# One plain fp32 weight tile at each norm in place of two, and a later start for GpSimd's rows

## The reference, cut to what matters

```python
for l in range(DEPTH):                                   # DEPTH = 2
    h = layer_norm(ALPHA * h + 0.5 * swiglu(h, ffn1_gate[l], ffn1_up[l], ffn1_down[l]), ln_g[l, 0], ln_b[l, 0])
    z = h @ w_in[l]
    ...
    mix = jnp.concatenate([y_conv, y_rec, y_pool], axis=-1) @ w_out[l]
    h = layer_norm(ALPHA * h + mix, ln_g[l, 1], ln_b[l, 1])
    h = layer_norm(ALPHA * h + cross_attn(h, mem, ca_q[l], ca_k[l], ca_v[l], ca_o[l]), ln_g[l, 2], ln_b[l, 2])
    h = layer_norm(ALPHA * h + 0.5 * swiglu(h, ffn2_gate[l], ffn2_up[l], ffn2_down[l]), ln_g[l, 3], ln_b[l, 3])
```

## Time and profile before

| | |
|---|---|
| runs | 2506.68, 2508.70, 2508.75 us, median 2508.7 |
| the profiled execution | 2508.65 us, span 2506.9 us |
| TensorE busy | 2435.2 us, 97% |
| VectorE, ScalarE, GpSimd busy | 1107.7, 827.6, 211.9 us |
| granted TensorE clock, mean | 0.99 of full speed |

### The profile page before, as it was taken

How to read it: one execution, slowest core, us unless ns; L and a number is a source line. 1 busy time by engine, 2 the same in 40 slices (tenths; PEclk the granted TensorE clock), 3 DMA queues, 4 the chain that set the end, 5 groups by cost and what they waited for, 6 DMA issues and landing times. The chain is left out here.

```text
span 2506.9 us, 36308 instructions
## 1 busy us (share of the span) xinstructions
PE 2435.2 (97%) x15029; PEld 1790.5 (71%) x15029; DVE 1107.7 (44%) x1434; ACT 827.6 (33%) x955; POOL 211.9 (8%) x100
## 2 busy tenths in 40 slices
PE   8999999999999999999999999999999999999996
PEld 8999988999999998899999954444444444444442
DVE  4557766644645867654578741112111111212112
ACT  4344344433433434433446411212222211222120
POOL 0002402200200331110020010000000000000001
PEclk9999999999999999999999999999999999999997
DMA  7665454565565545456455557999999999999990
GB/s 241 210 202 168 136 184 151 169 202 181 172 201 172 169 149 185 134 186 202 152 182 166 165 209 315 428 427 430 428 428 428 429 429 428 430 427 429 428 423 18
DMA packets 215307, 665.16 MB, mean 265 GB/s; under 512 B 9841, under 2 KB 164207, under 8 KB 190624
## 3 DMA queue, kind: packets, MB, share of 16 engines
q1 hardware_dynamic: 214912, 662.53, 69.5%
q10 hardware_dynamic: 288, 1.05, 0.1%
HBM read 662.50 MB, written 1.05 MB: 265 GB/s over the span
## 5 line engine op out<-in xcount | busy, mean ns | idle before, releaser
L598 PE MATMUL ps<-ring_halves 128*128 128x256 f32 x5984 | 753.3, 284 | 0.0
L598 PEld LDWEIGHTS ps<-ring_halves 128*128 128x128 f32 x5984 | 734.2, 192 | 3.5 <-issue 0.6
L1803 DVE TENSOR_TENSOR ring_halves<-ring,ring_halves 128x2048 fp32r<-128x2048 f32 x206 | 511.5, 2491 | 360.9 <-ACT ring_halves L1320 360.8
L1320 ACT CAST ring_halves<-ring 128x2048 fp32r<-128x2048 f32 x206 | 391.2, 1903 | 276.1 <-PE ps L598 141.6
L1192 PE MATMUL ps<-ring,work 128*64 128x512 f32 x2048 | 452.3, 596 | 22.8 <-DMA ring<-in_w_up_dram 22.0
L1308 ACT COPY work<-ps 128x512 f32<-128x512 f32 x190 | 109.6, 586 | 840.9 <-PE ps L1192 390.7
L1192 PEld LDWEIGHTS ps<-ring,work 128*64 128x64 f32 x2048 | 145.8, 137 | 323.3 <-issue 269.5
L2305 DVE TENSOR_SCALAR work<-work 128x128 f32<-128x128 f32 x64 | 19.3, 344 | 610.1 <-PE ps L1192 610.1
L609 PE MATMUL ps<-ring_halves,work_halves 128*128 128x512 f32 x1184 | 288.4, 391 | 0.0
L2424 POOL TENSOR_TENSOR h<-hn,work 128x1024 f32<-128x1024 f32 x20 | 79.6, 3980 | 2084.9 <-DVE hn L1843 1052.9
L609 PEld LDWEIGHTS ps<-ring_halves,work_halves 128*128 128x128 f32 x1184 | 219.7, 188 | 44.4 <-issue 0.5
(11 more groups left out here) (257 smaller groups left out, 1736.0 us busy)
## 6 DMA issues: line engine op xcount, KB each, us to landing
ring<-in_w_up_dram SPq DMA_DIRECT2D x128, 2048.0 KB, 23.7
ring<-in_w_down_dram SPq DMA_DIRECT2D x64, 2048.0 KB, 19.3
ring<-in_w_in_dram SPq DMA_DIRECT2D x52, 1024.0 KB, 5.2
ring<-in_ffn_gate_dram SPq DMA_DIRECT2D x44, 1024.0 KB, 5.4
ring<-in_ffn_up_dram SPq DMA_DIRECT2D x44, 1024.0 KB, 5.3
ring<-in_ffn_down_dram SPq DMA_DIRECT2D x44, 1024.0 KB, 4.9
ring<-in_w_out_dram SPq DMA_DIRECT2D x12, 1024.0 KB, 4.9
ring<-in_ca_k_dram SPq DMA_DIRECT2D x8, 1024.0 KB, 5.1
```

The lines of the kernel that those rows point to most:

```text
L598: mm = pe.matmul(ps[:, bank, pt * T:pt * T + T], wt[:, o:o + P], x[:, k, :], start=(k == 0 and n == 0), stop=(k == DT - 1 and n == 2))
L1320: nc.scalar.copy(high_of(name)[:], ring[:, s, :]).then_inc(hi_done.add(name), 1)
L1803: v.tensor_tensor(ring_halves[s][:], ring[:, s, :], high_of(name)[:].bitcast(F32), ALU.subtract)\
```

## The change

At each of the eight norms only tile a is left in plain fp32. Tile b (`rf1`, `cq1`, `up 0`, `xa1`) joins the split tiles: it gets its place at the head of the order, ScalarE and VectorE prepare it, and TensorE multiplies it by `by_columns` after both halves are there. The first feed-forward stage of layer 0, which has no norm before it, keeps its way. GpSimd's rows wait for the low half of tile b and no longer for the split of the inputs.

```diff
+ORDER_MIX1 = ("rf1", "rq0", "rq1", "cc", "ch", "cb", "pu", "ri0", "ri1", "ck0", "ck1", "ck2", "ck3", "rg0", "rg1",
+              "cv0", "cv1", "cv2", "cv3", "wo0", "wo1", "wo2", "wo3", "cq1", "cq2", "cq3", "co0", "co1", "co2", "co3")
+ORDER_MIX2 = ("xa1", "xa2", "xa3", "q0", "q1", "k0", "k1", "v0", "v1", "v2", "v3", "go0", "go1", "go2", "go3",
...
-    out = []
+    out = [] if tag == ("f1", 0) else [(tag, "up", 0)]
...
                 half(a_name, a_bank, 0, (0, 1))
-                open_bank(b_bank, b_name)
-                arrived(b_name)
-                half(b_name, b_bank, 0, (0,))
                 transposes(tag, 1, hn)
-                half(b_name, b_bank, 0, (1,))
                 turned_copied(tag, 1)
                 release(half(a_name, a_bank, 1, (0, 1)), a_name)
-                release(half(b_name, b_bank, 1, (0, 1)), b_name)
+                split_inputs(tag)
+                by_columns(b_name, b_bank)
...
                     slot_used(act, (f"rf{j}", L))
                     nc.scalar.activation(work[:, FQ + 512 * j:FQ + 512 * j + 512], ps[:, j, :], ACT.Sigmoid)\
                         .then_inc(emptied[j].sem, 1)
+                next_high(("rf1", L))
...
                 mine(("k", L))
+                next_low(("rf1", L))
                 next_low(("rq0", L))
                 next_low(("rq1", L))
...
                 negmax(1)
+                next_low(("cq1", L))
                 next_low(("cq2", L))
                 normalise(1)
...
             conv(0)
+            next_low("xa1")
             next_low("xa2")
...
                 if tag[0] not in ("A", "B"):
-                    pool.wait_ge(dve_done.sem, dve_done.at(("xlow", tag, 1)))
+                    n, L = tag
+                    second = {0: ("rf1", L), 1: ("cq1", L), 2: (("f2", L), "up", 0),
+                              3: (("f1", L + 1), "up", 0) if L + 1 < LAYERS else "xa1"}[n]
+                    pool.wait_ge(lo_done.sem, lo_done.at(second))
```

More of the change, by code:

```diff
@@ L156, in join @@
             ln.n = n
-ORDER_MIX1 = ("rq0", "rq1", "cc", "ch", "cb", "pu", "ri0", "ri1", "ck0", "ck1", "ck2", "ck3", "rg0", "rg1",
-              "cv0", "cv1", "cv2", "cv3", "wo0", "wo1", "wo2", "wo3", "cq2", "cq3", "co0", "co1", "co2", "co3")
-ORDER_MIX2 = ("xa2", "xa3", "q0", "q1", "k0", "k1", "v0", "v1", "v2", "v3", "go0", "go1", "go2", "go3",
+ORDER_MIX1 = ("rf1", "rq0", "rq1", "cc", "ch", "cb", "pu", "ri0", "ri1", "ck0", "ck1", "ck2", "ck3", "rg0", "rg1",
+              "cv0", "cv1", "cv2", "cv3", "wo0", "wo1", "wo2", "wo3", "cq1", "cq2", "cq3", "co0", "co1", "co2", "co3")
+ORDER_MIX2 = ("xa1", "xa2", "xa3", "q0", "q1", "k0", "k1", "v0", "v1", "v2", "v3", "go0", "go1", "go2", "go3",
               "mb0", "mb1", "mb2", "mb3", "ga0", "ga1", "ga2", "ga3", "ma0", "ma1", "ma2", "ma3")
 def ffn_order(tag):
-    out = []
+    out = [] if tag == ("f1", 0) else [(tag, "up", 0)]
     for c in range(1, 9):
@@ L721, in ffn @@
                     first_pair(before, (((tag, "gate", 0), 0), ((tag, "up", 0), 1)))
-                split_inputs(before)
+                if opening:
+                    split_inputs(before)
                 def gate_up(c):
@@ L816, in mix @@
                 first_pair((0, L), ((("rf0", L), 0), (("rf1", L), 1)))
-                split_inputs((0, L))
                 by_columns(("rq0", L), 2)
@@ L915, in cross_attention @@
                 first_pair((1, L), ((("cq0", L), 2), (("cq1", L), 3)))
-                split_inputs((1, L))
                 scores(0)
@@ L950, in _ @@
             first_pair((3, LAYERS - 1), (("xa0", 0), ("xa1", 1)))
-            split_inputs((3, LAYERS - 1))
             by_columns("xa2", 2)
@@ L1396, in ffn @@
                 silu(0)
+                if not opening:
+                    next_high((tag, "up", 0))
                 hidden(0)
@@ L1535, in cross_attention @@
                 expo(0)
+                next_high(("cq1", L))
                 q_copy(2)
@@ L1575, in _ @@
                 copy_out(j, xa[:, 2 * j:2 * j + 2, 3:259], ps[:, j, :].rearrange("p (g t) -> p g t", g=2))
-                if j >= 2:
+                if j >= 1:
                     next_high(f"xa{j}")
@@ L1900, in ffn @@
                 up(0)
+                if not opening:
+                    next_low((tag, "up", 0))
                 hidden(0)
```

## The result

The changed kernel takes 2544.3 us in the median (2544.08 to 2545.78) beside 2508.7 us for the kernel before: a ratio of 1.0146, 95% interval 1.0131 to 1.0161. It is slower, by 35.6 us. The profiled execution took 2544.19 us.

The account below looks back on a forecast made before the run. TensorE, busy 2435.2 of 2506.9 us, was taken as the bound. Norms 26.6, mixing stages 2, `q0` 0.3 and clock 4 summed to 33 us on 2508.65: about 2541 us, range 2532 to 2553.

Parts of the forecast that it names:

- Tile b covers the second norm chain, and the chain does not move: At each norm: without tile b's cover TensorE waits 2.40 us before the transposes and 1.95 us after them.
- The low half of tile b: After tile a's second half at each norm: TensorE waits 0.96 us for VectorE's low half.
- The clock, +4 us: TensorE's clock falls at some of the eight norms' new gaps, held briefly: 0.5 us a norm, +4 us.
- `cc` and `q0`, +2.3 us: Low halves come late: about 1 us in each of two mixing stages, 0.3 us for `q0` after the last norm.
- the lost cover: At the eight norms, new waits outweigh the 1.36 us of work saved: +3.33 us a norm, +26.6 us in all.
- POOL's turns: After each norm POOL and VectorE alternate; only the third subtraction meets POOL, and the first low half gains nothing.
- The clock holding: Rival: TensorE's clock holds at all norms, total 2537.7 us; chance 35%.
- The clock falling at nearly all norms: Rival: the clock falls at nearly all norms, 2.6 us each, total 2559 us; chance 10%.
- The faster one: Rival: second-half rows are ready when tile a's first half ends, so 1.36 us a norm stay saved; 2497.8 us, 3%.
- made up in the experts' stage: Rival: the delay is made up later, as in the DMA-busy experts' stage; 2511 to 2532 us, 4%; no change 1%.

Follow-up runs that it names:

- The filled gaps: Changed kernel with useless plain fp32 matmuls of tile a in both idle gaps of each norm; 2536.4 us, ratio 1.0119.
- the late plain kernel: Kernel before with tile b still in plain fp32, but all of it moved behind tile a's second half; 2551.5 us, ratio 1.0174.
- reordered kernel: Changed kernel with the second half's sums, square root and scaling put before the split of the first half's inputs; 2517.0 us, ratio 1.0036.
- the two kernels with POOL's wait undone: Changed kernel, and the half split, each with POOL waiting for the split of the inputs instead of tile b's low half; 2545.7 and 2505.6 us.
- the half split: Changed kernel with the second norm chain put ahead and only 128 of tile b's columns split, the others plain fp32; 2505.1 us, ratio 0.9986.

## Why the prediction held

It was 2541 us, with 2532 to 2553 around it, and 2544.3 was measured. By its steps:

- **Tile b covers the second norm chain, and the chain does not move.** Right: the transposes start at A+5.97 in the earlier trace rows and in the trace after. The waits were forecast at 2.40 and 1.95 us, and are 2.16 and 1.59; tile a's first half is 3.81 us to its end where I had set 32 x 0.1116 = 3.57, and the copies are seen by TensorE sooner than with the 0.25 us I allowed. The filled gaps, where the clock is out of play, put tile b at A+13.26 for the forecast A+13.35, and cost 28.0 us for the forecast 28.9.
- **The low half of tile b.** Right in mechanism: 0.79 us for 0.96. In the changed kernel itself this wait does not exist, as TensorE is later than VectorE.
- **The clock, +4 us.** This is the term that was mis-sized. It fell at eight norms of eight, and costs 1.50 us at the first norm (14.76 against 13.26) and 1.34 in the mean, 10.7 us for the forecast 4. I had set each piece of idle time against the single gap of 2.62 us that did no harm, and that row is not a rule. The same gap stands in all eleven traces of this case; behind it the clock is low in six of them and high in five, the kernel before and the changed one among the five. So a piece of 2.16 us is within what can lower the clock by itself, as the second norm of the late plain kernel shows. With only the second piece, 1.59 us, the clock holds at every norm. Whether the two pieces together make the fall so regular (eight of eight) is not settled: no run has the first piece without the second.
- **`cc` and `q0`, +2.3 us.** Nearly nothing in the changed kernel (0.4 us). The slow clock had given VectorE the time. The forecast 1 us a stage shows itself where the clock holds: 0.8 us in the filled and in the reordered kernel, and 1.9 where the norm is shorter still. The sum came out within 3.3 us partly by luck: the clock cost 6.7 us more than forecast, the low halves 1.9 less and the lost cover 0.7 less, and the norms then account for 37.0 us where the medians differ by 35.6.
- **POOL's turns.** Right: three subtractions in 8.89 us for 11.06, the first unchanged. The forecast that it gains TensorE nothing is shown twice, by the two kernels with POOL's wait undone. The Trainium skill's rule (SBUF — State Buffer, "two separate sides"), that the one of the two engines which starts first holds the shared ports for its whole instruction, fits these rows as it did.
- **The rivals.** The clock holding was wrong. The clock falling at nearly all norms, given 10%, is what happened; its price was wrong, 2.6 us a norm for 1.34. Tile a's second half was over after 6.1 us at the first norm (211.96 to 218.09) and not after 7.1, as the clock came back within it, and a part of the loss was hidden in the wait for the low half, as forecast. So the range was met by a milder form of a rival that the prediction had put beyond it. The faster one needed the scaled rows by the end of tile a's first half. The kernel with the chain ahead has just that, and is still 8 us slower than before, because the copies and the low half remain to be waited for. Nothing was made up in the experts' stage.

## What to carry to other kernels

Work that looks dear by its own duration may be the cover of a chain on other engines. Before replacing it by something cheaper that has to come later, lay the new order against the chain's fixed times and count what stays uncovered; here 1.36 us of saving stood against 4.6 us of new waiting at each of eight places, before the clock is counted. If the chain can be shortened, do that first and then trade the cover for cheap work only as far as the shorter chain allows: half a tile, not all of it. A queue that was uncritical at one pace has to be read again at the next, as the low half of `cc` shows.

## What the hardware showed that I had not expected

- Two idle pieces of 2.16 and 1.59 us around 0.90 us of transposes lowered TensorE's clock to 1.2 GHz each of eight times, for 3.4 or 6.8 us. 0.90 us of transposes and 1.59 us of idle time after it lowered it at none of eight, in the kernel with the chain ahead.
- Whether a single gap lowers the clock can change from one execution to the next. A gap of 2.62 us did in six traces of eleven, and in one of two executions of the same program; gaps of 1.96 and 1.94 us did in one kernel, and gaps of 1.87 us did not in its twin. The low clock behind such a gap costs 1.4 and 1.5 us in the two rows above. The mean clock of the kernel before varies as well: of its 27 runs beside the half split, the seven below 2507 us have 0.990 and the four above 2511 us 0.987. At which gaps it fell in those, no trace shows.
- Useless matmuls in idle time made the kernel 8 us faster, by keeping the clock up.
- The start of the kernel varies by about 2 us between executions: TensorE reached the first norm at 205.27 us in the profiled execution of before, and between 202.8 and 205.0 in the others. The whole difference lies in one product, TensorE's first, of which these are the rows of the kernel before and of the changed one:

```profile
10.07 16.12 PE L706 MATMUL ps<-hT,ring 128*128 128x256 f32 x64 [1.09 <-DVE hT L1817]
...
10.20 14.05 PE L703 MATMUL ps<-hT,ring 128*128 128x256 f32 x64 [1.09 <-DVE hT L1816]
```

  From 10 to 14 us the kernel before starts 9 of these 64 rows and the changed one 18; from 14 to 18 us both start 19 or 20. That is half the pace, as at 1.2 GHz. The windows give 1.00 for the clock there, but the traces hold no record of it before 14.26 us (before) and 9.11 us (changed), and in each of the eleven traces a first record after 12.9 us goes with a first norm after 204.4, and one before 9.5 us with a first norm before 203.4.
